# Value projection with tokens on partitions in a one-core decoder layer on Trainium2

## The reference

```
z = x @ w_in + b_in                     # 2048 x 6664
za, ga, q, k, v, zf, gb, zc, gc, zg = split(z)
y_a = pool_mixer(za) * silu(ga)         # 256 channels
y_b = attention(q, k, v, zf) * silu(gb) # 8 heads of 64; logits += F[t] - F[s],
                                        # F = cumsum(log_sigmoid(zf)), zf is 2048 x 8
y_c = s5_mixer(zc) * silu(gc)           # 256 channels; a complex scan over time
merged = sum over 3 branches of sigmoid(zg_branch) * (y_branch @ w_up_branch)
out = LayerNorm(alpha * x + merged @ w_out)
```

## Time and profile before

| | |
|---|---|
| median of three runs | 1897.27 us (1897.17 to 1897.75) |
| the profiled execution (its span; the page gives no other time) | 1897.9 us |
| mean granted TensorE clock | 0.998 |
| PE busy | 1880.5 us, 10349 instructions |
| DVE, ACT, POOL busy | 1123.9, 720.4, 450.8 us |
| chain that ended last | PE 17% of the span, in the merge's tail; DVE 1% |
| scan by POOL, hf 0 | 148.9 to 248.4 us |

### The profile page before, as it was taken

The page is one execution under the profiler, slowest core; times in us unless marked ns, Lnnn a source line. Parts: engine busy times, 40 slices in busy tenths (PEclk is TensorE's granted clock), DMA queues, the critical chain, the costliest instruction groups (busy, mean ns, idle before and its releaser), DMA issues. The chain is left out here.

```text
span 1897.9 us, 30532 instructions
## 1 busy us (share of the span) xinstructions
PE 1880.5 (99%) x10349; PEld 1611.9 (85%) x10349; DVE 1123.9 (59%) x2370; ACT 720.4 (38%) x1105; POOL 450.8 (24%) x595
## 2 busy tenths in 40 slices
PE   9999999999999999999999999999999999999998
PEld 7888887888887888888888788888888889999997
DVE  5554225564235665746656675565656688766776
ACT  3121013111024565555545655555555542121111
POOL 2948920399000000010100001000010002223322
PEclk9999999999999999999999999999999999999999
DMA  7132235322432143161432714224152486666542
GB/s 197 67 101 89 88 111 186 80 89 89 151 128 100 63 128 85 45 158 57 126 82 68 228 51 133 77 77 131 49 153 74 157 294 199 189 180 183 166 133 89
DMA packets 111335, 230.22 MB, mean 121 GB/s; under 512 B 11544, under 2 KB 61320, under 8 KB 107640
## 3 DMA queue, kind: packets, MB, share of 16 engines
q1 hardware_dynamic: 96752, 168.69, 27.7%
q0 software_dynamic: 13920, 59.46, 11.9%
q10 hardware_dynamic: 576, 1.05, 0.2%
HBM read 159.29 MB, written 69.27 MB: 120 GB/s over the span
## 5 line engine op out<-in xcount | busy, mean ns | idle before, releaser
L1628 PE MATMUL g_ps<-x_hi,w_hi 128*128 128x512 f32 x768 | 305.9, 398 | 0.0
L1628 PE MATMUL g_ps<-x_hi,w_lo 128*128 128x512 f32 x768 | 305.6, 398 | 0.0
L1543 DVE TENSOR_TENSOR pt_lo<-t_ps,pt_hi 128x512 fp32r<-128x512 f32 (+2 forms) x320 | 193.2, 610 | 150.0 <-ACT pt_hi L1419 145.3
L1628 PE MATMUL g_ps<-x_lo,w_hi 128*128 128x512 f32 x768 | 231.7, 406 | 1.2 <-PEq L1664 1.2
L1419 ACT ACTIVATE pt_hi<-t_ps 128x512 fp32r<-128x512 f32 (+2 forms) x320 | 170.6, 533 | 154.8 <-PE t_ps L1584 149.2
L763 PE MATMUL tile_ps<-x_hi,w_hi 128*128 128x512 f32 x720 | 223.7, 392 | 0.1
L763 PE MATMUL tile_ps<-x_hi,w_lo 128*128 128x512 f32 x720 | 221.8, 389 | 0.0
L763 PE MATMUL tile_ps<-x_lo,w_hi 128*128 128x512 f32 x720 | 221.8, 389 | 0.0
L1306 POOL DMA_DIRECT2D mixT<-y_out x63 | 33.8, 536 | 678.5 <-DVE y_out L1487 601.0
L1584 PE MATMUL t_ps<-ident,s_sb 128*128 128x128 f32 x1088 | 173.1, 274 | 2.5 <-DVE v_st L1528 2.5
L1464 DVE CUSTOM_DVE_ANT_0 s_sb<-s_ps,f_row 128x512 f32<-128x512 f32 (+3 forms) x288 | 161.1, 597 | 15.0 <-PE s_ps L1573 15.0
(11 more groups left out here) (319 smaller groups left out, 3595.5 us busy)
## 6 DMA issues: line engine op xcount, KB each, us to landing
w_lo_raw<-in_w_tiles SPq DMA_DIRECT2D x95, 512.0 KB, 3.7
gateT<-g_out SPq DMA_DIRECT2D x96, 256.0 KB, 3.0
gate<-gateT SPq DMA_DIRECT2D x62, 384.0 KB, 4.7
qkvT<-zout SPq DMA_DIRECT2D x24, 512.0 KB, 3.2
x_lo_raw<-in_xT SPq DMA_DIRECT2D x20, 512.0 KB, 9.7
silT<-zout SPq DMA_DIRECT2D x16, 512.0 KB, 2.7
k_ll<-qkvT POOLq DMA_DIRECT2D x16, 512.0 KB, 7.3
q_st<-qkvT POOLq DMA_DIRECT2D x16, 512.0 KB, 9.2
```

The lines of the kernel that those rows point to most:

```text
L1543: dve.tensor_tensor(pt_lo[part], t_ps[n % 2][:, 0:keys].rearrange("p (k q) -> p k q", q=P), pt_hi[part].bitcast(F32), ALU.subtract).then_i ...
L1628: mm = pe.matmul(g_ps[c][:], w[j % 2][:, k, :], x[:, k, c * BANK:(c + 1) * BANK], start=(r == 0), stop=(r == 3 * KT - 1))
```

## The change

V's four tiles of each half and the forget logits are taken out of their places and computed with the roles of the operands exchanged: x is stationary (128 tokens of it), the weights stream. For each group of 128 tokens there is one product of 264 columns (256 channels of V and the 8 forget channels, from the new input w_vf) and one of 256 (the other half of V, from two ordinary weight tiles side by side), 24 matmuls each. DVE adds the bias, as the bias now differs by column (sum_v), SP stores 128 x 256 to vS, whole, with tokens as rows. The 8 forget columns of each token tile are copied and turned by 8 transposes in each half. This block (values) stands between the za tiles and the gated tiles, V's tiles having stood at the end of the half. The first two gated tiles get weights of their own buffers (b_hi, b_lo), since w_hi and w_lo hold V's. In attention POOL loads a head's V from vS straight into v_st, split over 16 groups of 128 tokens; the transposes go, ACT copies and DVE subtracts on the loaded data.

```diff
-T_ZC, T_ZA, T_SIL, T_QKV, T_GATE = 2, 2, 8, 12, 24
-T_SIL0 = T_ZC + T_ZA
...
+T_V0 = T_ZC + T_ZA
+T_SIL0 = T_V0 + T_V
...
+PAIR = 2 * P
...
+TOK = HALF // P
...
+        def v_ps(i):
+
+            return tile_ps[(i // 2) % 2][:, (i % 2) * BANK:(i % 2) * BANK + (PAIR if i >= TOK else PAIR_F)]
...
                     rows = io["xT"][k * P:(k + 2) * P].rearrange("(k p) t -> p k t", p=P)
                     sp.dma_start(x_raw[:, k:k + 2, BANK:HALF], rows[:, :, BANK:HALF]).then_inc(x_late[k // 2], 16)
+            def load_values():
+
+                sp.dma_start(vb_raw[:].rearrange("p k c -> p (k c)"), io["w_vf"]).then_inc(vb_loaded, 16)
+                sp.dma_start(v_bias[:], io["b_v"].partition_broadcast(P)).then_inc(v_bias_in, 16)
+
+            def store_v(hf, i):
+
+                sp.wait_ge(v_sums, 2 * TOK * hf + i + 1)
+                tok, part = hf * HALF + (i % TOK) * P, i // TOK
+                sp.dma_start(scr["vS"][tok:tok + P, part * PAIR:(part + 1) * PAIR],
+                             v_sum[i % 2][:, 0:PAIR]).then_inc(v_stored[i % 2], 16)
+
...
                         chunks = scr["zcT"].rearrange("(g h) (f t c) -> f t h g c", h=GC, f=2, t=TAU)
                         for t in range(TAU):
                             sp.dma_start(u_sb[GC * t:GC * (t + 1)], chunks[hf, t]).then_inc(u_loaded, 16)
-                with sp.Fori(0, T_SIL // 2) as i:
+                for i in range(TOK - 1):
+                    store_v(hf, i)
+                sp.wait_ge(v_done, 2 * TOK * hf + TOK)
+                sp.wait_ge(w_split, n0 + T_SIL0)
+                for u in range(2):
+                    sp.dma_start(b_raw[u][:], row(T_SIL0 + u)).then_inc(w_loaded[u], 16)
+                for i in range(TOK - 1, 2 * TOK - 1):
+                    store_v(hf, i)
+                sp.wait_ge(tile_done, n0 + T_SIL0)
+                sp.wait_ge(w_split, n0 + T_SIL0 + 2)
+                for u in range(2):
+                    load_w(row(T_SIL0 + 2 + u), u)
+                store_v(hf, 2 * TOK - 1)
+                for u in range(2):
+                    store(scr["silT"][u * P:(u + 1) * P], hf, u, n0 + T_SIL0 + u)
+                with sp.Fori(1, T_SIL // 2) as i:
                     for u in range(2):
                         sp.wait_ge(tile_done, i * 2 + (n0 + T_SIL0 + u + 1))
...
                     act.wait_ge(disc_arg, 2)
                     act.activation(sn[:], red[:], ACT.Sin).then_inc(disc_act, 1)
                     act.activation(sh[:], red[:], ACT.Sin, scale=0.5).then_inc(disc_act, 1)
+                act.wait_ge(vb_loaded, 16 * (hf + 1))
...
+                    act.wait_ge(aux_full, uses["v", 1] + 4)
+                act.activation(vb_hi[:], vb_raw[:], ACT.Copy).then_inc(vb_high, 1)
                 for i in range(2):
                     split_w(i, 8 * n0 + 48)
+                for u in range(2):
+                    act.wait_ge(w_loaded[u], 8 * (n0 + T_SIL0) + 16)
+                    act.activation(b_hi[u][:], b_raw[u][:], ACT.Copy).then_inc(w_split_hi, 1)
+                act.wait_ge(v_sums, 2 * TOK * (hf + 1))
                 with act.Fori(0, T_SIL // 2) as i:
                     for u in range(2):
...
+            def sum_v(hf, i):
+
+                width = PAIR if i >= TOK else PAIR_F
+                if i >= 2 or hf == 1:
+                    dve.wait_ge(v_stored[i % 2], 16 * (TOK * hf + i // 2))
+                dve.wait_ge(v_done, 2 * TOK * hf + i + 1)
+                dve.tensor_tensor(v_sum[i % 2][:, 0:width], v_ps(i), v_bias[:, (i // TOK) * PAIR_F:(i // TOK) * PAIR_F + width],
+                                  ALU.add).then_inc(v_sums, 1)
+                dve.wait_ge(v_sums, 2 * TOK * hf + i + 1)
+                done = dve.nop()
+                done.then_inc(tile_out if i in (2 * TOK - 3, 2 * TOK - 1) else v_free, 1)
+                if i < TOK:
+                    dve.tensor_copy(f_tok[:, i, :], v_sum[i % 2][:, PAIR:]).then_inc(f_copied, 1)
+
+            def values(hf):
+
+                n0 = hf * T_HALF
+                dve.wait_ge(v_bias_in, 16 * (hf + 1))
+                if hf == 1:
+                    dve.wait_ge(z_stored[1], 8 * (T_SIL + T_QKV))
+                for i in range(2 * TOK):
+                    sum_v(hf, i)
+                    if i in (TOK, TOK + 2):
+                        u = (i - TOK) // 2
+                        dve.wait_ge(w_split_hi, n0 + T_SIL0 + u + 1)
+                        dve.tensor_tensor(b_lo[u][:], b_raw[u][:], b_hi[u][:].bitcast(F32),
+                                          ALU.subtract).then_inc(w_split, 1)
+                    if i == TOK + 3:
+                        forget_logits(hf)
             def state_inputs(hf):
...
                     split_w(i, n0 + i + 2)
...
                 pooling_input(0)
...
                     state_inputs(1)
+                dve.wait_ge(vb_high, hf + 1)
+                dve.tensor_tensor(vb_lo[:], vb_raw[:], vb_hi[:].bitcast(F32), ALU.subtract).then_inc(vb_split, 1)
+                split_w(0, n0 + 4)
                 pooling_input(1)
                 split_w(1, n0 + 5)
+                values(hf)
...
             def forget_logits(hf):
...
-                pe.wait_ge(f_split, 1)
+                pe.wait_ge(f_copied, TOK * (hf + 1))
                 for c in range(NCH):
                     ps = open_bank("f", hf, c)
+                    for t in range(4):
+                        last = pe.transpose(ps[0:HEADS, t * P:(t + 1) * P], f_tok[:, 4 * c + t, :], ident[:])
+                    last.then_inc(aux_full, 1)
+
+            def values(hf):
+
+                n0 = hf * T_HALF
+                pe.wait_ge(vb_split, hf + 1)
+                for i in range(2 * TOK):
+                    if i in (0, 2):
+                        pe.wait_ge(tile_out, n0 + T_V0 - 1 + i // 2)
+                    elif i >= 4:
+                        pe.wait_ge(v_free, (2 * TOK - 2) * hf + i - 3)
+                    if i == TOK:
+                        pe.wait_ge(w_split, n0 + T_SIL0)
+                    tok = slice((i % TOK) * P, (i % TOK + 1) * P)
+                    out = v_ps(i)
                     for k in range(KT):
-                        for j, x in enumerate((x_hi, x_lo)):
-                            last = pe.matmul(ps[:], wf_st[:, k, :], x[:, k, c * BANK:(c + 1) * BANK],
-                                             start=(k == 0 and j == 0), stop=(k == KT - 1 and j == 1))
-                    last.then_inc(aux_full, 1)
+                        if i < TOK:
+                            hi, lo = vb_hi[:, k, :], vb_lo[:, k, :]
+                        else:
+                            hi, lo = w_pair_hi[:, :, k, :], w_pair_lo[:, :, k, :]
+                            out = v_ps(i).rearrange("p (b c) -> p b c", b=2)
+                        for j, (x, w) in enumerate(((x_hi, hi), (x_hi, lo), (x_lo, hi))):
+                            last = pe.matmul(out, x[:, k, tok], w, start=(k == 0 and j == 0), stop=(k == KT - 1 and j == 2))
+                    last.then_inc(v_done, 1)
+                    if i == TOK + 1:
+                        forget_logits(hf)
+                pe.wait_ge(v_done, 2 * TOK * (hf + 1))
+                pe.nop().then_inc(tile_done, 2)
             def state_inputs(hf):
...
                     project(0, n0, True)
                     pe.wait_ge(tile_out, n0)
                 project(1, n0 + 1, halves=hf == 0)
-                forget_logits(hf)
...
                     if hf == 1 and i == 0:
                         state_inputs(1)
+                values(hf)
+                for u in range(2):
+                    pe.wait_ge(tile_out, n0 + T_SIL0 + u - 1)
+                    project(u, n0 + T_SIL0 + u, w_hi=b_hi, w_lo=b_lo)
+
...
                 if hf == 0:
-                    gated_tiles(0, 2)
+                    gated_tiles(1, 2)
                     in_tables()
                     gated_tile(2, 0)
                     kernels()
...
-                    gated_tiles(0, 3)
+                    gated_tiles(1, 3)
...
 W_SPLIT_AT = {1: 4, 5: 8, 9: 10, 12: 14}
...
-PT_USES = 2 + S_PIECES
+PT_USES = S_PIECES
...
                     pool.dma_start(k_ll[half].bitcast(F32), scr["qkvT"][bass.ds(q_row + D_B, HD)]).then_inc(kq_loaded, 16)
...
-            def load_v(q_row):
-                pool.dma_start(vT[:], scr["qkvT"][bass.ds(q_row + 2 * D_B, HD)]).then_inc(v_loaded, 16)
+            def load_v(column):
+                pool.dma_start(v_st[:, :, HD:].bitcast(F32), v_rows[:, :, bass.ds(column, HD)]).then_inc(v_loaded, 16)
             def load_f(h):
...
                 stored(h9 * 16 + 16 * n)
             pool.sem_inc(y_free, 2)
+            for u in range(2):
+                pool.wait_ge(kept.v_stored[u], 2 * 16 * TOK)
+            load_v(0)
             for u in range(2):
                 pool.wait_ge(kept.z_stored[u], 8 * 2 * (T_SIL + T_QKV))
             with pool.Fori(0, HEADS - 1) as h:
                 pool.wait_ge(s_full, h * S_PIECES + S_PIECES)
                 load_kq(h * HD + HD)
```

(38 more changed lines are left out.)

99 lines of the change are left out of this document (50 added, 49 removed).

## The result

The changed kernel takes 1910.89 us (median of 4 runs, 1909.93 to 1911.64) against 1897.51 for the kernel before (4 runs, 1897.17 to 1900.26): 1.0067 times the time before, 95% interval [1.0053, 1.0081], slower by 13.4 us. In a second set on one chip it came to 1911.87, ratio 1.0069 [1.0056, 1.0083]. The forecast was 1911.0. The profiled execution took 1911.64 with a span of 1910.1; single executions of the changed kernel stand some 1.5 us above their spans, and differ among themselves by as much. By the two profiled spans the change is +12.2 (1910.1 against the 1897.9 of before). That is somewhat too small: in the 27 executions of the kernel before that were timed beside the experiments the time stands 1.9 us above the span and the spans go from 1894.7 to 1898.4, median 1895.7, so the profile of before is of one of its slower executions, by some 2 us.

What follows compares the result with a forecast made beforehand. PE, busy 99% of the span, was taken as the bound, each new wait added in full. Terms -5.8 - 9.1 + 22.0 + 1.7 + 3.9 + 1.7 - 0.5 = +13.9 on 1897.27 gave 1911 us, range 1901 to 1922.

Steps and rivals of the forecast that it cites:

- The scan: hf 0: y products on PE wait for POOL's scan, as four tiles of cover are gone; +22.0 us.
- The clock behind it: After the scan stall in hf 0 the granted clock falls from 2.4 GHz to the level of 1.2; +1.7 us.
- hf 1's load: hf 1: PE wants u_sb for the state inputs before its load lands; +3.9 us, and +1.7 of clock.
- Products: Both halves: narrow products replace V's tiles and the forget logits, with 16 transposes and two short waits; -5.8 us.
- Transposes: Attention: the 16 transposes of V, 1.14 us in each of 8 heads, go; -9.1 us.
- Head 4: Change of phase: the v_st wait goes, but V's load may delay PE's fills; -0.5 us, between -3.4 and +4.
- V by head: Attention: each head's V load lands about 10 us after issue, within the margin; 0 us for all eight.
- Rival B: hf 0: the scan costs PE nothing and the kernel is faster, 1887 us; chance 0.07.
- C: Attention: V lands late in every head, 24 us after issue, from 256-byte packets; 1969 us; chance 0.05.
- D: hf 0: the scan itself slows to hf 1's 112.9 us, +13.4, giving 1924 us; chance 0.10.
- head 0's margin: Attention, head 0: how late V may land after issue before PE suffers; 14.6 us.
- the scan's upper bound of 35: hf 0: the largest PE stall for the scan, in us, taken from hf 1's 112.9 us scan.

Runs made afterwards that it cites:

- e1: Changed kernel with the scan of hf 0 lacking its second sweep (its values are then wrong): 1890.4 us, ratio 0.9964 to the kernel before.
- e3: Changed kernel with input tables, kernels and state inputs two tiles earlier in hf 0, pooling sums ahead of them: 1890.43 us, ratio 0.9960 to the kernel before.
- e9: The changed kernel once more, unaltered, on one chip with e10 and e11: 1911.87 us, ratio 1.0069 to the kernel before.
- e4: Changed kernel with hf 1's state inputs in the middle of the second za tile instead of ahead of it: 1910.97 us, ratio 1.0069 to the kernel before.
- e6: Changed kernel with sixteen unused 64x64 identity transposes put back at the start of each head: 1919.91 us, ratio 1.0110 to the kernel before.
- e7: Changed kernel with V's load for a head issued as two DMAs of 32 columns: 1909.84 us, ratio 1.0066 to the kernel before.
- e11: Changed kernel with hf 1's state inputs mid second za tile and the 264-column weights' split between the state-input copies: 1905.62 us, ratio 1.0040 to the kernel before.
- e5: Changed kernel with 84 identity products on PE during hf 0's wait for the scan: 1910.29 us, ratio 1.0063 to the kernel before.
- e10: Changed kernel with 88 identity products on PE during hf 0's wait for the scan: 1909.17 us, ratio 1.0058 to the kernel before.
- e2: Changed kernel with 150 identity products on PE during hf 0's wait for the scan: 1924.18 us, ratio 1.0137 to the kernel before.
- e8: e3 plus, in hf 1, state inputs mid second za tile and the 264-column weights' split between their copies: 1883.52 us, ratio 0.9919 to the kernel before.

## Why the prediction was right, step by step

**The scan** carried it: 22.0 us forecast, 20.3 measured (19.0 to 20.3 in the profiles of this order). Cover less than the chain behind the state inputs, worked out from two rows, gave it within 2 us. The scan took 97.5 us instead of 99.45 and started 17.1 after the state inputs instead of 16.3: 17.1 + 97.5 + 0.1 = 114.7, less the cover of 94.3 (173.35 to 267.68; 94.1 forecast). e1 and e3 show the cause in two ways: a shorter scan and an earlier one both take 20.5 us off by the runs.

**The clock behind it** was priced too low: 1.7 forecast, 3.0 measured in the first profile (33.71 less 30.70), 1.8 in that of e9 (32.5 less 30.7). In the six profiles with this wait (the changed kernel, e4, e6, e7, e9, e11) the clock stayed at 0.50 for 3.6 to 6.1 us of work, and y to GLU took 32.5 to 33.7 us. I had priced it from the one gap of the trace before, of 2.54 us, where the clock recovered within about 4 us at 0.63 and 0.52. So one profile gives such a price to about 1 us only, and 1.7 lies just below the range of 1.8 to 3.0. e5 and e10 confirm the cause locally (30.8 and 30.7 us).

**hf 1's load**: 3.9 + 1.7 forecast, 4.3 measured, and 6.2 for both together when e11 takes them away. Here too the low clock lasted between 3.2 and 6.1 us of work, in the nine profiles that have this wait. The trace of before held all that was needed: when the load's transfers end, and when PE now wants them.

**Products**: -5.8 forecast. In hf 0 50.77 - 47.56 = 3.2, so -6.4 for both halves; 264 columns cost 0.1208, not 0.1235: interpolating by columns was too dear by 1.0 us.

**Transposes**: -9.1 forecast; e6 gives them back at +9.0 by the medians (8.2 by the two ratios to the kernel before), +9.5 by the spans.

**Head 4**: -0.5 forecast. Of the 10.5 us that seven heads gained, 8.0 are transposes, 2.5 is left for it. The wait of 2.54 us and the low clock went, and three short ones came, of 0.42, 0.47 and 1.30 us (the longest for w_lo, of the gates' weights); none of them lowers the clock in this profile. The timeline of PE in the changed kernel:

```profile
1091.52 0.50 PE L1745 MATMUL g_ps<-x_lo,w_hi 128*128 128x512 f32 x1 [0.42 <-DVE x_lo L1633]
1094.81 0.32 PE L1699 MATMUL t_ps<-ident,s_sb 128*128 128x128 f32 x1 [0.47 <-ACT s_sb L1515]
1097.02 2.10 PE L1745 MATMUL g_ps<-x_lo,w_hi 128*128 128x512 f32 x8 [1.30 <-DVE w_lo L1564]
```

The row of ACT just before says where they come from:

```profile
1090.11 0.63 ACT L1509 ACTIVATE x_hi<-x_lo_raw 128x512 fp32r<-128x512 f32 x1 [2.66 <-DMA x_lo_raw<-in_xT]
```

ACT waits for the last pieces of x_lo_raw and is done with them at 1092.47. Behind that stand, in the order of ACT and DVE, the first exponents of head 4 (PE's wait of 0.47) and the split of the gates' weights (1.30). So PE waited 2.2 us for this chain in all, within the 4 us allowed, and 1.1 instead of 0.42 for x_lo in e9. V's load of this head, issued at 1079.2, is under way at the same time; ACT waited for x_lo_raw before the change too (2.6 us in all), and no run takes the two apart. Nor is the price of these waits always their own length: in e2, e4 and e8 the clock did fall behind the one of 1.3 us. In e8:

```profile
1068.28 0.49 PE L1762 MATMUL g_ps<-x_lo,w_hi 128*128 128x512 f32 x1 [1.30 <-DVE w_lo L1581]
...
1068.00:1070.00 2.00, 1.72 (x5) 1.40 (x6) 1.97 (x13) 0.94 (x3) 0.00 (x0) 0.67 0.81 138
1070.00:1072.00 2.00, 2.00 (x7) 1.51 (x6) 1.39 (x4) 1.18 (x2) 0.00 (x0) 0.50 0.12 42
```

**V by head**: 0 forecast, and no wait for it in the view. Its landing I had at 10 us, it is 5.6 in the median and 10.7 at head 4. I took the time by the number of packets, and counted 2048 of 256 bytes where the trace has 128 of 4096. By bytes the u_sb row would have given it: u_sb moves 8 x 128 KB = 1 MB, V half of that, and 8.2/2 + 1.5 = 5.6, though one row does not make a rule. A nearer row was there: the old load of V, 512 KB on the same queue in rows of 8 KB, landed after 4.7 us (8.6 at head 4). So the new load takes 0.9 us longer than the old one, or 2.1 at head 4. The rule of the Trainium skill named in the forecast (DMA: Bandwidth & Descriptors, Specifications) is neither borne out nor refuted by this: its 8.2 us or more did not come, 5.6 us for runs of 256 bytes and 5.5 for 128, but no packet of V in the trace is under 512 bytes.

**The sum** was +13.9; by the milestones it is 17.8 + 3.0 + 2.3 - 10.5 - 0.4 = +12.2 of span (the 2.3 between GLU and the end of head 0: -3.2 for the second V block, +4.3 and 1.7 for u_sb, -1.1 for one head's transposes, 0.6 unassigned), and 13.4 by the medians. The first term, 17.8, is the wait of 20.3 less 3.2 for the first V block, with 0.7 unassigned. The errors are -1.7 (scan), +1.3 (clock), -0.6 (products), -2.0 (head 4) and +0.4 (u_sb with its clock); with 0.9 us unassigned they make the 1.7 by which the sum is above the spans. That the medians land within 0.1 us of the forecast is luck; the terms are right to 2 us each. The 0.6 us that I left as noise between span and median was in truth a time 1.9 us above the span and a profile of a slow execution, two things that cancel in part.

Rival B (the scan costs nothing) fell with the wait of 20.3 us; C (V late, 24 us after issue) with landings of 5.5 to 10.7; D (the scan slows to 112.9) with 97.5. Two figures of the forecast don't fit together, without bearing on the result: with its own terms head 0's margin is some 14 us and not 14.6, and the scan's upper bound of 35 gives 1924, outside the range that names it. PE's busy time fell by 13.4 us (some 14 forecast), and its idle time grew by 25.6 (26 forecast).

## What to carry to other kernels

Where one engine is busy 99% of the time, moving work of it is not free even if its amount falls: every chain on another engine that runs in the shade of that work loses the cover. List, for each such chain, when its result is ready and when it is wanted, and take off what is moved from between the two; the chain's start can then be moved with the work, as e3 does, which turned a loss of 13 us into a gain of 7, and with e11's part into one of 15.

A second wait often stands behind the first (e4): before moving a consumer later, follow what else starts only when it is done, through every engine's own order.

## What the runs showed of the hardware

The granted clock fell from 1.00 to 0.55 within the second stretch of 2 us of idleness (268 to 272). After waits of 19.0 to 20.3 us it stayed at 0.50 for 3.6 to 6.1 us of work in six profiles, and after waits of 3.8 to 4.4 us for 3.2 to 6.1 in nine: the length of the wait made no difference that can be told from that between executions. Filling the wait with identity products held it at 1.00 (e2, e5, e10). The wait of 1.6 us at the start of attention left it alone in all profiles of the new order; that of 1.3 us at head 4, which follows shorter ones, left it alone in nine of twelve profiles and was followed by a fall to 0.50 for 3.4 us in e2, e4 and e8.

POOL's 112 instructions of a scan took 97.5 us beside 24.8 us of DVE work, 99.6 beside 30.3 (e3) and 112.9 beside 65.6. No run changed the DVE work alone.

Matmuls of 256 and 264 columns stood 0.1198 and 0.1208 us apart, 512 columns 0.2267 (before the change): the 256-column form costs 5.7% more per column, so splitting one 512-column product in two is dearer by 0.013 us, and the gain of the new form lay in the 8 columns that ride along for 0.001 us.
